# Both halves' bias products of a mixture-of-experts block at one place, the second half's opening its sums

## The reference, cut to what matters

```
def expert_block(args):
    xb, e = args
    hid = xb @ w1[e] + b1[e]                    # 1024 -> 2048
    return clamped_swiglu(hid) @ w2[e] + b2[e]  # 1024 -> 1024

def clamped_swiglu(hid):
    x_glu = jnp.minimum(hid[..., ::2], SWIGLU_LIMIT)
    x_lin = jnp.clip(hid[..., 1::2], -SWIGLU_LIMIT, SWIGLU_LIMIT)
    return x_glu * jax.nn.sigmoid(SWIGLU_ALPHA * x_glu) * (x_lin + 1.0)
```

## Time and profile before

| | us |
|---|---|
| median of 3 runs | 1646.26 |
| lowest and highest | 1645.65, 1648.67 |
| the profiled execution, its own time | 1652.45 |
| its span, from the first to the last instruction | 1650.6 |

### The profile page before, as it was taken

How to read it: one execution, slowest core, us unless ns; L and a number is a source line. 1 busy time by engine, 2 the same in 40 slices (tenths; PEclk the granted TensorE clock), 3 DMA queues, 4 the chain that set the end, 5 groups by cost and what they waited for, 6 DMA issues and landing times.

```text
span 1650.6 us, 20381 instructions
## 1 busy us (share of the span) xinstructions
PE 1573.1 (95%) x6973; PEld 1078.9 (65%) x6973; DVE 1287.8 (78%) x1063; ACT 995.6 (60%) x888; POOL 145.0 (9%) x116
## 2 busy tenths in 40 slices
PE   5999899986899999999999999999999999999987
PEld 3887655553566666666666666666666666666656
DVE  3423233238699999999999999999999999999885
ACT  5423222133477777777777777777777777777632
POOL 5000000002620000000000000000000000000030
PEclk9999688897899999999999999999999999999979
DMA  4128300043799999999999999999999999999951
GB/s 158 51 102 289 138 14 1 13 154 105 261 372 384 366 372 379 374 377 368 367 363 381 377 376 374 368 362 373 374 384 373 370 368 369 372 372 380 374 201 51
DMA packets 130687, 479.00 MB, mean 290 GB/s; under 512 B 9187, under 2 KB 9734, under 8 KB 130662
## 3 DMA queue, kind: packets, MB, share of 16 engines
q1 hardware_dynamic: 119222, 440.24, 71.9%
q0 software_dynamic: 6112, 21.52, 4.1%
q10 hardware_dynamic: 5328, 16.91, 2.7%
HBM read 453.21 MB, written 25.43 MB: 290 GB/s over the span
## 4 chain that ended last, share of the span: by engine, by line
PE 89%; DVE 5%; issue 2%; ACT 2%; DMA 1%; POOL 0%; ACTq 0%; SPq 0%; POOLq 0%; DVEq 0%
PE ps L1118 42%; PE ps L1143 22%; PE ps L949 8%; PE ps L964 4%; PE ps L1127 2%; PE ps L1009 1%; PE ps L1106 1%; PE ps L1150 1%; DVE HL L1480 1%; PE ps L1086 1%; PE ps L1031 1%; PE ps L1217 1%; PE ps L983 1%; DVE H L1555 1%; PE ps L903 1%
## 5 line engine op out<-in xcount | busy, mean ns | idle before, releaser
L1480 DVE TENSOR_TENSOR HL<-W,HL 128x2048 fp32r<-128x2048 f32 x384 | 876.0, 2296 | 75.1 <-ACT HL L741 67.6
L741 ACT ACTIVATE HL<-W 128x2048 fp32r<-128x2048 f32 x384 | 734.9, 1915 | 222.8 <-PE ps L1118 123.5
L1118 PE MATMUL ps<-HL,XTh 128*96 128x512 f32 x2048 | 566.4, 398 | 8.1 <-DVE XTl L1476 4.9
L1118 PEld LDWEIGHTS ps<-HL,XTh 128*96 128x96 f32 x2048 | 324.9, 163 | 141.1 <-issue 5.4
L1118 PE MATMUL ps<-HL,XTl 128*96 128x512 f32 x1024 | 321.2, 395 | 0.0
L1143 PE MATMUL ps<-HL,HIDTh 128*96 128x512 f32 x1024 | 285.9, 401 | 2.6 <-DVE HIDTl L1505 2.6
L1143 PEld LDWEIGHTS ps<-HL,HIDTh 128*96 128x96 f32 x1024 | 160.7, 162 | 83.6 <-issue 15.0
L1118 PEld LDWEIGHTS ps<-HL,XTl 128*96 128x96 f32 x1024 | 165.8, 162 | 71.8 <-issue 0.5
L1143 PE MATMUL ps<-HL,HIDTl 128*96 128x512 f32 x512 | 160.8, 396 | 0.0
L551 POOL DMA_INDIRECT XG<-f_rows,tokix x33 | 64.8, 1963 | 999.6 <-PE ps L1106 998.1
L1143 PEld LDWEIGHTS ps<-HL,HIDTl 128*96 128x96 f32 x512 | 82.8, 162 | 36.0
(11 more groups left out here) (256 smaller groups left out, 1454.6 us busy)
## 6 DMA issues: line engine op xcount, KB each, us to landing
W<-in_w_dram SPq DMA_DIRECT2D x384, 1024.0 KB, 8.3
wst<-in_w_in_dram SPq DMA_DIRECT2D x6, 2048.0 KB, 8.0
y_rows<-actT ACTq DMA_DIRECT2D x32, 384.0 KB, 6.1
y_rows<-M SPq DMA_DIRECT2D x1, 8448.0 KB, 41.9
H<-in_x_dram SPq DMA_DIRECT2D x8, 512.0 KB, 6.4
wst<-in_w_out_dram SPq DMA_DIRECT2D x2, 2048.0 KB, 16.8
W<-in_w_ple_gate_dram SPq DMA_DIRECT2D x4, 1024.0 KB, 8.1
f_rows<-M ACTq DMA_DIRECT2D x4, 512.0 KB, 2.9
```

The lines of the kernel that those rows point to most:

```text
L741: act.activation(HL[:, k % HRING, 0], w_slot(k), ACT.Copy).then_inc(w_hi, 1)
L1118: last = pe.matmul(ps[0:CAP, 2 * h + n], xt[:, c], HL[:, s, part, cc * 1024 + n * 512:cc * 1024 + (n + 1) * 512], start=(c == 0 and xt is ...
L1480: dve.tensor_tensor(HL[:, k % HRING, 1], w_slot(k), HL[:, k % HRING, 0].bitcast(F32), ALU.subtract).then_inc(w_lo, 1)
```

## The change

TensorE now multiplies both halves' biases after chunk 3. The first half's two products close their sums, as before. The second half's two products open theirs, in banks 2 and 3, before chunks 6 to 9 add to them. The place after chunk 9 falls away. In the loop the second pair waits for `htl_out`, because bank 2 held the turned rows of the block before. Whoever waited for the bias of the second half (the clamp of the second half, the copy into `XTh`) waits for chunk 9 in `piece_used`. `sel` may be overwritten as soon as the products of the block before have counted `b1_done` (the new name of `h1_done`) twice.

```diff
             def split_x(b):
                 act.wait_ge(xt_done, b + 1)
                 if not first_block(b):
-                    act.wait_ge(h1_done, b * 2)
+                    act.wait_ge(piece_used, chunks(b - 1, 9))
...
             def choose_bias(b):
...
-                    act.wait_ge(h1_done, b * 2)
+                    act.wait_ge(b1_done, b * 2)
...
                             last = pe.matmul(ps[0:CAP, 2 * h + n], xt[:, c], HL[:, s, part, cc * 1024 + n * 512:cc * 1024 + (n + 1) * 512],
-                                             start=(c == 0 and xt is XTh and part == 0), stop=False)
+                                             start=(h == 0 and c == 0 and xt is XTh and part == 0),
+                                             stop=(h == 1 and c == NC - 1 and xt is XTl))
...
-            def add_b1(b, h):
-                if h == 0:
-                    pe.wait_ge(sel_ready, b + 1)
-                for n in range(2):
-                    rows = slice(n * 2 * NE, (n + 1) * 2 * NE)
-                    last = pe.matmul(ps[0:CAP, 2 * h + n], sel[rows, :], BB[rows, h * 512:(h + 1) * 512], start=False, stop=True)
-                last.then_inc(h1_done, 1)
+            def add_b1(b):
+
+                pe.wait_ge(sel_ready, b + 1)
+                for h in range(2):
+                    if h == 1 and not first_block(b):
+                        pe.wait_ge(htl_out, b * 2)
+                    for n in range(2):
+                        rows = slice(n * 2 * NE, (n + 1) * 2 * NE)
+                        last = pe.matmul(ps[0:CAP, 2 * h + n], sel[rows, :], BB[rows, h * 512:(h + 1) * 512], start=(h == 1), stop=(h == 0))
+                    last.then_inc(b1_done, 1)
...
                 w1_chunk(b, 3)
-                add_b1(b, 0)
+                add_b1(b)
...
                 w1_chunk(b, 9)
-                add_b1(b, 1)
...
             def clamp(b, h):
 
-                dve.wait_ge(h1_done, b * 2 + (h + 1))
+                if h == 0:
+                    dve.wait_ge(b1_done, b * 2 + 1)
+                else:
+                    dve.wait_ge(piece_used, chunks(b, 9))
```

More of the change, by code:

```diff
@@ L318, in hybrid_layer @@
         piece_used = sem("piece_used")
-        h1_done = sem("h1_done")
+        b1_done = sem("b1_done")
         moe_step = sem("moe_step")
```

## The result

The median of four runs is 1637.29 us, against 1647.47 us for the kernel before in four runs; the ratio over the runs is 0.9932 with a 95% interval of 0.9903 to 0.9961 (the two medians alone give 0.9938). By the medians the changed kernel is faster by 10.2 us, and 1636.0 was forecast from a base of 1646.26. Its profiled execution took 1643.24 us, with a span of 1641.4, 9.2 us less than the span before.

A forecast was written before the change was run, and what follows sets the result against it. The prediction took TensorE to bound the kernel. Removed pairs 17.8 us, less added pairs 7.2 and 0.3 in block 0, made 10.3 us off the median: 1636.0 us, range 1633 to 1642.

The forecast's parts named there:

- TensorE sets the pace: In the loop TensorE is busy 300.00 of 300 us and waits for nobody, so shortening its products shortens the time.
- The removed pair at 0.575 us: Bias pair after chunk 9: removing it saves 0.575 us a block, 0.233 of streaming and 0.34 of row change.
- The added pair at 0.233 us: Second bias pair directly behind the first, after chunk 3: costs only the plain pitch of one product, 0.233 us.
- the first rival: At the second bias pair after chunk 3: it costs 0.40 us, not 0.233, giving 1641.2 us; chance 0.12.
- The net of a block, 0.34 us: Per loop block, removed pair less added pair: 0.575 - 0.233 = 0.34 us saved, 35.90 becoming 35.56.
- The wait for `htl_out`: Ahead of the second pair in the loop: the condition is met 4.3 us early, so the wait costs nothing.
- VectorE's 2.1 us to give: VectorE works 33.8 us of a 35.90 us block, leaving 2.1 us to spare where 0.34 is asked.
- The ends of the sum: First and last blocks: 0.3 us taken back in block 0; the end hangs on chunk 5 of the last block.
- Each pair leaving the array first: At the two pairs after chunk 3: the first leaves before the second enters, which costs 0.40 us; chance 0.12.
- Nothing saved: The second pair pays entry and exit again, or VectorE takes the gain back: 1645 to 1647 us; chance 0.08.
- The weight loads as the bound: In the loop, landings grow past 12.4 us and ScalarE, VectorE, then TensorE wait: slower, 1651 us; chance 0.04.

The follow-up runs named there:

- the 128-row products: The kernel before, its four bias products at their old places but over all 128 rows: 35.65 us a block, against 35.90.
- the first experiment: The changed kernel with the second bias pair moved behind chunks 4 and 5, ahead of chunk 6, so two places again: 35.87 us a block, ratio 0.9999 to before.
- the two 128-row kernels: Bias products over all 128 rows, in the kernel before at the old places (35.648 us a block) and in the changed kernel side by side (35.614).
- three pairs: The changed kernel with the second half's bias added twice, so three bias pairs stand behind each other: 35.77 us a block, against 35.52.
- 128 rows side by side: The changed kernel with its four bias products over all 128 rows, still behind each other: 35.61 us a block, against 35.52.

## Why the prediction was right, point by point

**TensorE sets the pace.** Right. It is busy for 300 of 300 us in every kernel tried, down to 34.70 us a block, and what comes off its products comes off the block.

**The removed pair at 0.575 us.** Right: 0.58 in the timeline at the place. That most of it is the change of rows and not the work was an inference then; the 128-row products, dearer to stream and cheaper as a whole, show it.

**The added pair at 0.233 us.** Right: 2.21 us was forecast from pair to pair and 2.21 was measured. The 28 products of L932 were the right rows to lean on, though they were misread: four of their seven groups use one row half and three the other (`GC * (c % 2)`), so the tiles take 16 or 12 records each and not 14. The step on the busier tiles is then 1.69/16 = 0.11 us, and the conclusion stands. The rule of the Trainium skill that a weight load overlaps with products in flight only where the row group differs ("TensorE: Matmul & The Clock Gate", Part 3, What overlaps and what doesn't) was read as a cost of 0.40 us here. That is the condition of the first rival, which the prediction calls the second. It was not borne out: the second pair loads the same two row groups and costs one stream, 0.23 us.

**The net of a block, 0.34 us.** A little too small: it is 0.38. The 0.35 of the two places leave about 0.03 over, the same size as the remainder of the first experiment and as the difference between the two 128-row kernels (0.03 each). The plain six-product stretches of `w1` and `w2` take 1.37 to 1.41 us. In the block from 1002 us two of them are at 1.37 before, and in the changed block from 1000 us three. Why is not settled.

**The wait for `htl_out` and VectorE's 2.1 us to give.** Right: the condition was met 3.7 us early (4.3 was forecast), and moving the wait ahead of all four changed nothing.

**The ends of the sum.** Chunk 5 of the last block as the point on which the end hangs was right, with the 0.23 of its added pair. In the first block 0.1 us was gained where 0.3 was forecast: TensorE now waits 0.21 us there for `XTl`, which is ready at 453.61, and goes on at 453.67 where it was 453.78 before. Ahead of the first bias this execution was already 0.06 us later (425.66 against 425.60), so 0.17 came of the change. The forecast let TensorE start with `XTl`, and it starts 0.06 us behind it. Up to chunk 5 of the last block 11.24 us were gained against the 10.3 of the sum, mostly because a block gained 0.38 and not 0.34. The profiled execution then gave 2.0 back in its tail, so that its 9.2 is near the sum is luck. The medians say 10.2, but single runs of the changed kernel lie between 1634.46 and 1643.24 us and the interval of the ratio allows 6.4 to 16 us, so that the time came out within 1.3 us of the forecast is in part luck too. What bears the prediction out is the block: 2.21 and 1.39 us at the two places.

**The rivals.** Each pair leaving the array first: refuted by the second pair's 0.23 and by three pairs. Nothing saved: refuted. The weight loads as the bound: landings went from 8.3 and 11.2 us (median and longest) to 8.5 and 11.4, no wait for them appeared, and without any bias the loop still held.

## What to carry to other kernels

Products over 64 or 32 rows between products over all rows cost the change into and out of that use of the array, here 0.34 us, more than the 0.23 us of a pair's streaming. Put all of them that a loop turn has at one place, and let them open a sum if they can't close it; the order inside the group is free, but they should lie in different row groups. Where just two are left, the same products over 128 rows can be cheaper than over half of them: two took 0.47 us against 0.575. A single one was not tried.

## What the runs showed of the hardware that was not expected

Four 64-row products in the order half A, A, B, B take 0.70 us, as in A, B, A, B (0.71), while A, A, A, A take 1.17. What fits this is that the array pairs products of different row halves even when they are not neighbours in the program; no record names its product, so it is not shown directly.

Four products of 32 rows in four row quarters fill 0.47 us, no more than two of 64 rows.

A remainder of some 0.03 us a block is left over in three comparisons (changed, two places, 128 rows side by side), and no run here explains it.
